# Triangular mask of the decays written into the exponent by a second matrix product into the same PSUM bank, in place of GpSimd's multiplication by a mask

## The reference

```python
g = jnp.cumsum(log_a, axis=2)
diff = gh[..., :, None] - gh[..., None, :]
incl = jnp.tril(jnp.ones((CHUNK, CHUNK), dtype=bool))
strict = jnp.tril(jnp.ones((CHUNK, CHUNK), dtype=bool), k=-1)
m = jnp.einsum('bnihk,bnjhk->bnhij', k_beta, k) * jnp.exp(jnp.where(strict, diff, -jnp.inf))
...
qk = jnp.einsum('bnihk,bnjhk->bnhij', q, k) * jnp.exp(jnp.where(incl, diff, -jnp.inf))
...
v_new = uc - jnp.einsum('bihk,bhkv->bihv', wc, s)
o = jnp.einsum('bihk,bhkv->bihv', qc, s) + jnp.einsum('bhij,bjhv->bihv', ac, v_new)
s = s * jnp.exp(dl)[..., None, None] + jnp.einsum('bihk,bihv->bhkv', kc, v_new)
```

## Time and profile before

| | |
|---|---|
| median of 3 runs | 4828.52 us (4826.89 to 4831.43) |
| the profiled execution | 4828.48 us |
| its span, first to last instruction | 4826.4 us |
| PE busy | 4047.1 us (84%), 34010 matmul records |
| DVE busy | 2191.7 us (45%) |
| ACT busy | 994.2 us (21%) |
| POOL busy | 973.7 us (20%) |
| mean granted TensorE clock | 0.896 |
| the scan of layer 0 | 564.8 to about 1200 us |
| the scan of layer 1 | 2965 to about 3597 us |

### The profile page before, as it was taken

The page is one execution under the profiler, slowest core; times in us unless marked ns, Lnnn a source line. Parts: engine busy times, 40 slices in busy tenths (PEclk is TensorE's granted clock), DMA queues, the critical chain, the costliest instruction groups (busy, mean ns, idle before and its releaser), DMA issues. The chain is left out here.

```text
span 4826.4 us, 84581 instructions
## 1 busy us (share of the span) xinstructions
PE 4047.1 (84%) x34010; PEld 3165.5 (66%) x34010; DVE 2191.7 (45%) x4945; ACT 994.2 (21%) x1930; POOL 973.7 (20%) x1020
## 2 busy tenths in 40 slices
PE   5999768787769999999569997788868699999993
PEld 3444556665439999999444444566654499999993
DVE  3334165554555444444433332655536544444444
ACT  2233234333110000000123322433331100000001
POOL 0035044442210010000000440444412101000000
PEclk9999888788879999999779998887879799999997
DMA  7465323321538989998564654233224299988994
GB/s 256 161 225 189 90 62 86 75 47 43 183 110 239 269 247 256 261 258 254 159 229 150 232 182 102 62 72 72 56 74 157 99 271 260 261 254 256 263 260 154
DMA packets 822396, 836.63 MB, mean 173 GB/s; under 512 B 91800, under 2 KB 667352, under 8 KB 815868
## 3 DMA queue, kind: packets, MB, share of 16 engines
q1 hardware_dynamic: 740540, 711.23, 49.3%
q10 hardware_dynamic: 69856, 80.89, 5.0%
q0 software_dynamic: 11616, 38.94, 3.5%
HBM read 698.83 MB, written 132.10 MB: 172 GB/s over the span
## 5 line engine op out<-in xcount | busy, mean ns | idle before, releaser
L2341 PE MATMUL ffn_hb<-ffn_xT,ffn_w 128*128 128x144 f32 x8192 | 1092.1, 293 | 64.9 <-issue 52.3
L2341 PEld LDWEIGHTS ffn_hb<-ffn_xT,ffn_w 128*128 128x128 f32 x8192 | 1057.7, 196 | 73.7 <-issue 58.1
L442 PE MATMUL front_acc<-front_w,front_xmT 128*128 128x512 f32 (+2 forms) x2304 | 873.9, 539 | 26.5 <-DVE front_xmT L635 25.4
L442 PEld LDWEIGHTS front_acc<-front_w,front_xmT 128*128 128x128 f32 x2304 | 436.7, 191 | 450.2 <-issue 433.1
L2349 PE MATMUL ffn_acc<-ffn_hT,ffn_w 128*128 128x144 f32 x4096 | 548.8, 287 | 0.0
L2349 PEld LDWEIGHTS ffn_acc<-ffn_hT,ffn_w 128*128 128x128 f32 x4096 | 520.2, 190 | 0.8
L2389 ACT ACTIVATE ffn_en<-ffn_hb 128x144 f32<-128x144 f32 x256 | 74.6, 291 | 1574.0 <-PE ffn_hb L2341 1574.0
L2488 DVE TENSOR_TENSOR ffn_hT<-ffn_en,ffn_hb 128x144 f32<-128x144 f32 x256 | 77.8, 304 | 604.9 <-ACT ffn_en L2389 604.4
L2273 POOL DMA_INDIRECT ffn_xe<-scratch_xhat,ffn_g_idx x34 | 34.6, 1019 | 1469.0 <-DVEq L2443 1469.0
L2062 PE MATMUL mixer_acc<-mixer_wout,mixer_oT 128*128 128x512 f32 x576 | 254.3, 600 | 0.0
L2412 DVE TENSOR_SCALAR_CACHE_REDUCE ffn_junk<-ffn_row,ffn_pair 128x128 f32<-128x128 f32 (+2 forms) x324 | 245.5, 758 | 6.5 <-DVE ffn_yp L2461 5.1
(11 more groups left out here) (316 smaller groups left out, 5290.1 us busy)
## 6 DMA issues: line engine op xcount, KB each, us to landing
ffn_w<-in_w_e SPq DMA_DIRECT2D x768, 512.0 KB, 6.4
x_res<-in_w_mod SPq DMA_DIRECT2D x32, 1024.0 KB, 5.3
x_res<-scratch_proj SPq DMA_DIRECT2D x36, 768.0 KB, 6.5
scratch_proj<-front_out ACTq DMA_DIRECT2D x90, 256.0 KB, 2.1
ffn_row<-scratch_affT SPq DMA_DIRECT2D x36, 576.0 KB, 6.5
front_w<-in_w_mod SPq DMA_DIRECT2D x8, 2048.0 KB, 9.1
front_w<-in_w_in ACTq DMA_DIRECT2D x8, 2048.0 KB, 10.4
scan_qk<-scratch_qkv SPq DMA_DIRECT2D x16, 1024.0 KB, 10.1
```

The lines of the kernel that those rows point to most:

```text
L442: mm = pe.matmul(acc[:, U % 2, 0:size], xmT[:, k, t * P:(t + 1) * P], w[:, n % 2, k, 0:size], start=k == 0, stop=k == KD - 1)
L2341: mm = pe.matmul(hb[:, b, i * CAP:(i + 1) * CAP], w[:, r, k, :], xT[:, s, k, :], start=k == 0, stop=k == KD - 1)
```

## The change

`decays` on PE gives each bank two products in place of one. The first is the old one, but leaves the accumulation open; the second adds `cumB` by `wall`, and closes it. `wall` is a new 128 by 64 tile, read eight times over by a stride of zero. It holds -1000 beside the diagonal, such that its product with `cumB` is -1000 for every pair above the diagonal and 0 elsewhere; exp makes zeros of these. POOL's `mask` and the semaphore `mask_l` go. `masked_grams` waits for `E_a` instead. DVE makes `wall` once at the start of each scan, with a memset and two small products, waits included.

```diff
-        laM_l, mask_l, kend_l, Rk_l = (st.sem(x) for x in ("laM_l", "mask_l", "kend_l", "Rk_l"))
+        laM_l, wall_v, kend_l, Rk_l = (st.sem(x) for x in ("laM_l", "wall_v", "kend_l", "Rk_l"))
+        wall = st.sb("wall", [P, CH])
...
                 def decays(g, i):
                     pe.wait_ge(laM_l, g + 2)
+                    pe.wait_ge(wall_v, 2)
                     pe.wait_ge(qT_a, halves[g][i] + 2)
                     for j in range(2):
-                        mm = pe.matmul(pA[:, 2 * i + j, :], strB, PM[:, 16 * i + 8 * j:16 * i + 8 * j + 8, :].rearrange("p b i -> p (b i)"), start=True, stop=True)
+                        out = pA[:, 2 * i + j, :]
+                        pe.matmul(out, strB, PM[:, 16 * i + 8 * j:16 * i + 8 * j + 8, :].rearrange("p b i -> p (b i)"), start=True, stop=False)
+                        mm = pe.matmul(out.rearrange("p (b i) -> p b i", i=CH), cumB, wall[:].unsqueeze(1).to_broadcast([P, 8, CH]), start=False, stop=True)
                     mm.then_inc(D_p, 1)
...
-                def mask(g, i):
-                    pool.wait_ge(E_a, halves[g][i] + 2)
-                    x = dec[:, 2 * i:2 * i + 2, :].rearrange("p m (h i) -> p m h i", i=CH)
-                    for m in range(2):
-                        pool.tensor_tensor(x[:, m], x[:, m], m64.unsqueeze(1).to_broadcast([P, H, CH]), ALU.mult).then_inc(mask_l, 1)
-
...
-                    for i in range(len(halves[g])):
-                        mask(g, i)
...
-                    dve.wait_ge(mask_l, c + 2)
+                    dve.wait_ge(E_a, halves[g][m // 2] + 2)
...
+                dve.memset(wall[:], 0.0).then_inc(own, step())
+                dve.wait_ge(own, step.n)
+                dve.tensor_scalar(wall[0:CH, 0:CH - 1], ident[0:CH, 1:CH], -1000.0, None, ALU.mult).then_inc(own, step())
+                dve.tensor_scalar(wall[CH:P, 1:CH], ident[CH:P, CH:P - 1], -1000.0, None, ALU.mult).then_inc(own, step())
+                dve.wait_ge(own, step.n)
+                dve.sem_inc(wall_v, 1)
                 for x in (TT[:], RD[:], gA[:], beta[:, 0, 16:], PM[:, 16:]):
```

## The result

The changed kernel takes 4851.47 us (median of 9 runs, 4839.71 to 4864.04); the kernel before, run in turn with it, 4827.96 (9 runs, 4821.09 to 4832.08). The ratio is 1.0049 with a 95% interval of 1.0037 to 1.0062: by that slower by 23.7 us, between 18 and 30. Its profiled execution took 4856.64 us.

A forecast was written before the change was run, and what follows sets the result against it. The prediction took each group's path to run through PE's decays, `read_state`, VectorE's masked grams and `block_in`, then attention. Groups 1 to 4 add 27.4 us, group 0 1.4: 4828.5 + 28.8 = 4857.3 us, range 4846 to 4867.

The forecast's parts named there:

- Second product, 0.428 us a record, all on the path in groups 1 to 4: PE's decays: 8 added records a group, 3.43 us each group, 27.4 us over two layers.
- The rival with 0.592: PE's decays: each added record costs its full 0.592 us, 40.6 us in all, time 4869; chance 0.05.
- the estimate by the 216 ns: PE's added records at the skill's full-clock figure: about 14 us, time about 4842; not used for the sum.
- The mask worth nothing in groups 1 to 4: POOL's mask, hidden behind VectorE's queue: removal gains nothing; 5.03 us a group at most if that cover were gone.
- Group 0: PE's added records cost 1.71 us, VectorE's product beside the mask gives back 1.02; 1.4 us over two layers.
- Making `wall`, and the wait on `E_a`: nothing: Scan start: some 1 us hidden by PE's 4.36 us DMA wait; masked grams' new wait: nothing.
- The sum: Whole kernel: 27.4 + 1.4 = 28.8 us slower, 4857.3 us; chance 0.85.
- Rival D: Attention takes up part of the delay; named in the experiments. The prediction's like rival: 4830 or 4844, chance 0.07.
- The clock rival: Attention: added PE work keeps TensorE's clock up, giving back at most 64 us, time 4793; chance 0.03.
- My spread of 0.4 us a group: Group lengths vary by some 0.4 us, ten groups by up to 4 us; forecast holds 4850 to 4865.
- the sign of being wrong that the prediction named: Attention: the prediction is wrong if its mean clock moves by more than 0.03.

The follow-up runs named there:

- The bf16 product: Changed kernel with `wall` and its weights as bf16 for the second product alone: 4883.23 us, ratio 1.0116.
- both: Changed kernel with the second product kept and POOL's mask put back, masked grams waiting for it again: 4849.59 us, ratio 1.0043.
- mask twice: Kernel before the change, each mask product on POOL issued two times: 4845.46 us, ratio 1.0038.
- The second profiles: Repeat runs without a new edit: the changed kernel again, 4851.40 us, and the kernel before again, 4825.62 us in one run.
- wall twice: Changed kernel with the product by `wall` issued two times into each bank: 4876.04 us, ratio 1.0101.
- the larger doses: The kernels wall twice, 4876.04 us, and mask twice, 4845.46 us.
- those with pads: Kernels with tiny products, four PE instructions each, added at the end of PE's scan to lengthen the code: 4739.87 to 4872.53 us.
- 9 pads: Kernel before the change with nine tiny products (36 PE instructions) at the end of PE's scan: 4872.53 us, ratio 1.0091.
- with 12: Kernel before the change with twelve tiny products (48 PE instructions) at the end of PE's scan: 4739.87 us, ratio 0.9814.
- 10 pads more: Changed kernel with ten tiny products at the end of PE's scan (112 PE instructions added in all): 4850.49 us, ratio 1.0046.

## Why the prediction was right, and where not

The forecast was 4857.3 us, slower by 28.8; measured was slower by 23.7, with an interval of 18 to 30.

*Second product, 0.428 us a record, all on the path in groups 1 to 4.* Right: 3.43 us a group forecast, 3.44 from the decays to `read_state`, 3.43 in the dense stretch, and 3.44 once more for a second `wall`. The rival with 0.592 falls. So does the estimate by the 216 ns of the Trainium skill ("TensorE: Matmul & The Clock Gate", section "Back-to-back issue gap") for the fp32 product, whose two records stand 0.43 us apart each. The bf16 product, with the next start 0.21 us later, agrees with the figure.

*The mask worth nothing in groups 1 to 4.* Right, by "both". One detail was thin. I named VectorE's queue as the cover, and did not say how far it reaches; by "mask twice" it ends some 2.6 us behind the mask's present end. Had the mask been twice as long, the change would have come out nearly even in these groups (21.91 against 21.33).

*Group 0.* The VectorE product of 1.30 us is gone, as said; all its 18 records in the changed kernel (duration min, median, max):

```profile
L1753 DVE TENSOR_SCALAR x_res<-x_res,qss x18: 278/282/786, 583.5 to 3042.7; 128x128 f32<-128x128 f32 x18
```

Its products of 0.79 us and less stand late in the group, beside the substitution on POOL, where before has them too. Group 0's stretch grew by 1.2 us in layer 0 (33.63 to 34.84) and 1.4 in layer 1 (33.25 to 34.62). The term said 0.7 each. The second profiles have 33.98 and 34.35 before, 34.38 and 35.13 in the change, so this size is inside the scatter.

*Making `wall`, and the wait on `E_a`: nothing.* Right; VectorE's memsets moved 1.15 us and PE still waited 4.31 us for the keys' DMA.

*The sum.* 28.8 against 23.7: the interval takes in the forecast, and the 5 us between them are not explained. The same profiles show how far the parts can be told apart. Growth over the profile of before in us: the dense stretches of all groups, group 0 included; both scans, from the first `small` to the last instruction; the whole span:

| kernel | dense stretches | both scans | span |
|---|---|---|---|
| change | 26.8 | 33.6 | 28.1 |
| both | 29.5 | 31.6 | 30.8 |
| wall twice | 59.3 | 56.4 | 47.6 |
| mask twice | 30.2 | 21.9 | 18.5 |

In the change the groups 1 to 4 gave 24.2 of the 26.8; the 3.2 us short of 27.4 are before's two stretches at the lower clock. What is left between scans and span, -5.5 us in the change and -8.8 in "wall twice", lies where nothing was edited. The second profiles of the change and of before differ by 42.9 us, 32 of it in the scans and 11 outside them, so that part scatters by as much as the 5 us in question. With the larger doses the span grew by 12 us less than the stretches. Rival D may be part of that; it isn't shown.

*The clock rival.* I said that I'd be wrong if the attention's mean clock moved by more than 0.03. It does, from one stretch to the next in one profile, without a sign. Two in the change, group 1 of each layer, columns as in the earlier trace rows:

```profile
721.00:814.20 93.20, 73.93 (x1027) 57.47 (x1028) 45.53 (x65) 40.71 (x85) 37.82 (x61) 0.80 0.39 86
...
3132.80:3232.40 99.60, 81.28 (x1026) 63.18 (x1027) 45.08 (x65) 40.96 (x85) 38.09 (x61) 0.71 0.38 81
```

The same attention took 93.2 us at a clock of 0.80 and 99.6 at 0.71. The group is 114.9 and 121.3 us long, where before it was 113.31 and 112.91. The two profiles of each kernel, and those with pads, which stand behind this code, allow a comparison without any edit. Group 1's attention took in before 94.83 and 97.80 us (layer 0), 94.42 and 92.71 (layer 1), and in the change 92.99 and 92.72, 99.42 and 97.79. The kernels with pads widen that: layer 0 took 93.10 us with 9 pads and 99.64 with 12. The same attention so varies by up to 6.5 us with no code changed. My spread of 0.4 us a group, taken from two groups that happened to agree, was the step that was too thin, and the runs of the changed kernel spread over 24 us. In both pairs the change has this attention shorter in layer 0 and longer in layer 1. With 10 pads more it has 97.00 and 97.92, so only layer 1 keeps its sign. Whether the change moves the attention's clock, group by group or on average, stays open; the sign of being wrong that the prediction named can't tell, since before moves as much by itself.

*What the prediction didn't ask.* It took for granted that parts without an edit stay as they are. For the change that held: 52.0 us of gaps against 52.3. That it did is a matter of place, for 36 instructions would have cost 43 us more and 48 would have given 90 back, either of them more than the whole effect of the change.

## What to carry to other kernels

Work taken from an engine that others don't wait for gives nothing, whatever its busy time; look how far the cover reaches, by what stands ahead in the waiting engine's queue. A row of products on PE is priced by the distance of their starts in the trace, and moving a piece within the row that the next step needs as a whole gains nothing. In a program with a long loop, count the instructions that an edit adds ahead of it, and look at the waits "issue" at its return and the packets of code loading in every comparison (the gaps of 9 us and of 4 have the same 296 to 298 packets, so look at both), before any number is put down to the edit.

## What the runs showed that was not expected

- At a loop's return PE stood still for 4 to 5 us, 9 us or not at all (12 returns: 52, 107 and 0 us), by nothing but the number of PE instructions ahead of the loop. One, two or no packet of code loading started within the gap. The products just behind a gap were slower on top, at a granted clock of 0.66 in the case shown. Twelve tiny products, 48 instructions, made the kernel 1.9% faster [0.9799, 0.9829].
- A bf16 product of 512 columns is one record with the next start 0.21 us later; the fp32 one is two records with starts 0.43 us apart.
- A VectorE product beside a POOL product took 1.30 us instead of 0.28 and ended with it, in "both" as in before, and not where POOL's was gone. The Trainium skill ("SBUF — State Buffer") describes a port pair that the two engines share and that one of them holds for a whole instruction while the other blocks; this row agrees.
